# Keys and queries projected first, attention's parts laid between the gate's and u's projections of a tile

## The chip, the cores and the metric

The kernel runs on one core of one Trainium2 chip. The metric is the device time of one execution in microseconds; a time given for several runs is their median. The profiled execution is one more run, with its own time.

## The reference

Two layers (DEPTH = 2) work on 512 prompt rows and 64 sample rows of width 1024, in fp32. What matters here is the first half of a layer, the mixer:

```python
h = x @ w_in          # columns: q 512 | k 128 | v 128 | u 512 | gv 512
q, k = rope(q), rope(k)
a = sink_attention(q, k, v)      # 8 query heads, 2 key heads, head_dim 64, window of 128 + own chunk
b = gelu(u) * (tril(W_s[g]) @ LN(gelu(gv)) + bias[g])       # 4 groups of 128 channels, chunks of 128
mixed = concat(rms_norm(a), rms_norm(b)) @ w_o
x = layer_norm(ALPHA * x + mixed)
# then: router, 16 experts in 4 groups, top 2 in the best group, x = layer_norm(ALPHA * x + moe(x))
```

Besides both outputs, the rotated keys, the values and (for the samples) the normalised gate rows are returned.

## The kernel before

**Tiles.** Rows are five tiles of 128: four of the prompt, and one with the 64 sample rows and 64 rows of zeros. NT is 5. A weight matrix is streamed in units of 512 x 512 values (1 MB), four blocks of 128 rows each; for keys and values a unit is 512 x 256. A unit s goes to slot s % 4 of `raw` by a DMA of the SP queue. ScalarE rounds it to `w_hi` (`split_hi`, L376) and VectorE writes the remainder to `w_lo` (`split_lo`, L382). Every fp32 product is three matmuls in a faster format: hi*hi, hi*lo and lo*hi. So a tile's product with two units is 24 matmuls on 128x512 (`product`, L1469 to L1483). The left operand is treated in the same way: rows are transposed by TensorE (four transposes of 128x128 into one bank, `turn`, L1462 to L1467), ScalarE copies the bank to the hi part (L392), VectorE subtracts (L397).

**Units of a layer.** 0 and 1: gate (gv). 2 and 3: keys and values. 4 and 5: queries. 6 and 7: u. 8 to 11: w_o. Then six per expert.

**Order on TensorE.** `head` (L1498) turns the five tiles of x and projects the gate, tile by tile. Then, for all five tiles each, keys and values, queries, u (L1514 to L1516). Only then attention begins: the keys are turned (`kt0`, `kt1`), the gating matrices (`wst`), and a loop over t (NT + 3 rounds) staggers the tiles: `scores(t)`, `turn_queries(t + 1)`, the gating products (all in round 0), `output(t - 3)`, `weighted_values(t - 1)`, `turn_mixed(t - 2)`, `turn_x1(t - 3)`, with the router's logits two rounds behind. `output` is the product with w_o.

**Order on the others.** ScalarE and VectorE have their own lists in the same order, each strictly in sequence; an instruction that waits for a semaphore holds back all behind it. ScalarE: gelu of gate and u out of PSUM (L706), queries' hi part (`queries_out`), eight exponentials of 128x256 per tile (`exponentials`, L743), copies of the turned probabilities (`probs_out`), sums of squares, square roots. Changing between gelu, exponential and square root costs an ACT_TABLE_LOAD. VectorE: rotation of keys and queries (L978), statistics and norm of the gate (L1023 to L1062), `scores_out` (scale and mask, row maxima, L1078), `attention_out`, `gmlp_out` (one channel group of four tiles at a time), `rms_norm`, `mixed_out` (adding the w_o product to x), `layer_norm` (L1134), and the subtractions for every lo part.

**Banks and memory.** PSUM has eight banks, A to H; `fill_plan` (L64 on) counts which value fills which bank in which order, and every producer waits until the bank's last reader has freed it. Projections go round A to D. The transposed x (`xt_hi`, `xt_lo`) fills an arena that is reused, once projecting is over, for keys, split queries (`q_hi`, `q_lo`), two buffers of probabilities, the mask (a 128x3x256 tensor loaded by ScalarE's queue, L727) and others. The mixed rows' split parts (`mt_hi`, `mt_lo`) have one buffer, over the gate's rows.

**Queues of the DMAs.** SP issues the weight units in order. POOL issues the small tables at the start and per layer, stores keys and values, later gathers rows and scatters results for the experts.

The lines that hold the order of TensorE before:

```python
for g in (1, 2, 3):
    for t in range(NT):
        projection(l, g, t)
...
for t in range(NT + 3):
    if t < NT:
        scores(t)
```

Of the kernel before, what the change touches and what calls it, by code (L numbers as in the profile page):

```python
# [19 lines left out]
F32R = mybir.dt.float32r  # L20
# [42 lines left out]
def fill_plan():  # L63
# [13 lines left out]
    for g in range(4):  # L77
        for t in range(NT):
            fill(("proj", g, t), "ABCD"[(g * NT + t) % 4])
    fill("kt0", "E")  # L80
    fill(("qt", 0), "G")
    fill("kt1", "F")
    fill("wst", "H")
    for t in range(NT + 3):
        if t < NT:
            for j in range(4):
                fill(("s", t, j), "ABCD"[j])
        if t + 1 < NT:
            fill(("qt", t + 1), "H")
        if t == 0:  # L90
            for r in range(NT):
                fill(("gm", r), "GH"[r % 2])
        if 4 <= t < NT + 2:
            fill(("logit", t - 4), "H")
            fill(("turned logit", t - 4), "H")
        if t >= 3:
            for c in range(2):
                fill(("wo", c, t - 3), "AB"[c])
        if 1 <= t < NT + 1:
            for j in range(4):  # L100
                fill(("pt", t - 1, j), "EF"[j % 2])
            fill(("o", t - 1), "G")
        if 2 <= t < NT + 2:
            for h in range(2):
                fill(("mt", t - 2, h), "EF"[h])
        if 3 <= t < NT + 1:
            for h in range(2):
                fill(("rt", t - 3, h), "CD"[h])
    for t in (NT - 2, NT - 1):
        for h in range(2):  # L110
            fill(("rt", t, h), "CD"[h])
        fill(("logit", t), "H")
        fill(("turned logit", t), "H")
# [9 lines left out]
def build(nc, x_prompt, x_sample, cache_k, cache_v, w_in, sinks, gm_ln_g, gm_ln_b, gm_ws, gm_bs,  # L123
# [5 lines left out]
    with ctx:  # L129
# [10 lines left out]

        raw = sb("raw", [P, RB, 4, HALF])
        w_hi = sb("w_hi", [P, RB, 4, HALF], F32R)
        w_lo = sb("w_lo", [P, RB, 4, HALF], F32R)
        x = sb("x", [P, NT, D])
# [7 lines left out]
        small = sb("small", [P, 400])  # L152
# [6 lines left out]
        xt_hi = over(base_t, "xt_hi", [P, KT_N, ROWS], F32R)  # L159
        xt_lo = over(base_t, "xt_lo", [P, KT_N, ROWS], F32R, 4 * KT_N * ROWS)  # L160
        keys_hi = over(base_t, "keys_hi", [P, 7 * P], F32R)
        keys_lo = over(base_t, "keys_lo", [P, 7 * P], F32R, at=3584)
        q_hi = over(base_t, "q_hi", [P, 4, P], F32R, at=7168)
        q_lo = over(base_t, "q_lo", [P, 4, P], F32R, at=9216)
        probs = over(base_t, "probs", [P, 2, 4, 2, 256], at=11264)
        probs_t = over(base_t, "probs_t", [P, 2, 4, P], at=27648)
        mask = over(base_t, "mask", [P, 3, 256], at=31744)
        ws_t = over(base_t, "ws_t", [P, 4, P], at=34816)
        consts = over(base_t, "consts", [P, 3 * P + 46 + 8 * NT])
        x1_t = over(base_t, "x1_t", [P, KT_N, P], at=36864)  # L170

        logits_t = over(base_t, "logits_t", [NE, P], at=3584)
# [9 lines left out]
        mt_hi = over(base_m, "mt_hi", [P, KT_N, P], F32R, at=2 * QB)  # L182
        mt_lo = over(base_m, "mt_lo", [P, KT_N, P], F32R, at=2 * QB + 4 * D)
        squares = over(base_m, "squares", [P, HALF], at=2 * QB + 8 * D)
# [31 lines left out]
        w12, warm = sm(NT, 2), sm(3)  # L216

# [19 lines left out]
        in_slot = over(base_t, "in_slot", [P, 2, 2 * NT, P], BF16, at=11264)  # L237
# [32 lines left out]
        ws_in, mask_in, consts_in = sem("ws_in"), sem("mask_in"), sem("consts_in")  # L270
# [76 lines left out]
        def width(s):  # L347
            return 256 if s in (2, 3) else HALF
# [51 lines left out]
        def t_cols(buf, h, c):  # L400

            return buf[:, 4 * h:4 * h + 4, c * P:(c + 1) * P]
# [30 lines left out]
        def _(sp):  # L433
# [33 lines left out]
            with sp.Fori(0, DEPTH) as l:  # L467
                s = 0
                for c0, n in ((1280, HALF), (HALF, 256), (0, HALF), (768, HALF)):
# [3 lines left out]
                for c in range(2):  # L473
                    for k in range(2):
# [1366 lines left out]
```

## Time and profile before

| | us |
|---|---|
| median of 3 runs | 1302.72 |
| lowest and highest | 1291.38 and 1303.28 |
| the profiled execution, its own time | 1304.67 |
| its span, first to last instruction | 1302.7 |
| TensorE busy | 1061.4 |
| VectorE busy | 898.7 |
| ScalarE busy | 709.3 |

Times in the rows are microseconds from the start of the span. Layer 0's mixer takes from about 19 to 276 us, its experts to about 626; layer 1's mixer starts at about 645 and its experts end at 1260. In layer 1 the projections end at 757, the first w_o product starts at 803 and the last ends at 896.7. PE is TensorE, PEld its weight loads, DVE VectorE, ACT ScalarE, SP the queue of the weight units. PEclk is the granted clock of TensorE: 1.00 is 2.4 GHz, 0.50 is 1.2 GHz.

### The profile page before, as it was taken

The page shows a single profiled execution, that of the slowest core. Times are in us where ns is not written, and L with a number is a line of the kernel's source. Part 1 is how long each engine was busy: PE and PEld are TensorE (multiplying, and loading weights), DVE is VectorE, ACT ScalarE, POOL GpSimd, SP SyncE. Part 2 cuts the span into 40 slices and gives each one's busy share as a digit, 9 for nine tenths or more (in the row PEclk, how much of TensorE's full clock was granted, in tenths as well). Part 3 has the DMA queues.
Part 4 walks back from the last instruction along what each step waited for, and adds up shares of the span by engine and source line. Part 5 has one row for each costly group of instructions (what it writes and reads, how often), then busy time and mean ns, then how long its engine had stood idle before and what let it go on. Part 6 is the DMA issues. An engine that isn't in the chain of part 4 may idle for free.

```text
span 1302.7 us, 16517 instructions
## 1 busy us (share of the span) xinstructions
PE 1061.4 (81%) x5382; PEld 875.0 (67%) x5382; DVE 898.7 (69%) x1082; ACT 709.3 (54%) x857; POOL 222.5 (17%) x164
## 2 busy tenths in 40 slices
PE   4998789947699999998279987997369999999920
PEld 3887677736577777877169856875258787777810
DVE  2583764476588788786767556645667888888827
ACT  2423563254477677775432257522457787777722
POOL 3000000006121222210250000000431212111115
PEclk9999799967899999999589988998589999999975
DMA  9313100026799999998713202011297999999851
GB/s 294 131 71 98 66 33 24 33 81 222 248 373 360 359 358 367 363 359 306 281 49 137 85 13 81 17 41 69 80 327 269 367 376 372 369 382 372 312 189 56
DMA packets 115618, 273.22 MB, mean 210 GB/s; under 512 B 10016, under 2 KB 13056, under 8 KB 114400
## 3 DMA queue, kind: packets, MB, share of 16 engines
q1 hardware_dynamic: 98608, 227.36, 48.8%
q0 software_dynamic: 14336, 33.00, 7.2%
q10 hardware_dynamic: 2608, 12.06, 2.6%
q8 instruction: 33, 0.54, 0.2%
q14 instruction: 33, 0.27, 0.1%
HBM read 262.00 MB, written 25.22 MB: 220 GB/s over the span
## 4 chain that ended last, share of the span: by engine, by line
PE 36%; DMA 20%; DVE 16%; issue 13%; ACT 8%; POOL 3%; DVEq 2%; POOLq 1%; ACTq 0%; SPq 0%
DMA raw<-in_w_gate 15%; PE bankA L1477 8%; PE bankB L1477 8%; DVE w_lo L382 5%; ACT w_hi L376 4%; PE bankC L1477 4%; PE bankD L1477 3%; DVE xt_lo L397 3%; POOL slot_rows L605 2%; PE bankA L1686 2%; PE bankB L1686 2%; PE bankC L1709 2%; PE bankD L1709 1%; DVE x L1405 1%; DMA rows<-x_rows,idx 1%
## 5 line engine op out<-in xcount | busy, mean ns | idle before, releaser
L382 DVE TENSOR_TENSOR w_lo<-raw,w_hi 128x2048 fp32r<-128x2048 f32 x216 | 487.7, 2269 | 111.8 <-ACT w_hi L376 110.2
L376 ACT ACTIVATE w_hi<-raw 128x2048 fp32r<-128x2048 f32 x216 | 409.7, 1901 | 214.1 <-DMA raw<-in_w_gate 54.6
L1686 PE MATMUL bankA<-w_hi,xt_hi 128*128 128x512 f32 x256 | 103.0, 402 | 18.8 <-DVE xt_lo L397 18.8
L1686 PE MATMUL bankB<-w_hi,xt_hi 128*128 128x512 f32 x256 | 102.6, 401 | 0.0
L1686 PE MATMUL bankB<-w_hi,xt_lo 128*128 128x512 f32 x256 | 100.1, 391 | 0.0
L1686 PE MATMUL bankA<-w_hi,xt_lo 128*128 128x512 f32 x256 | 100.1, 391 | 0.0
L1686 PE MATMUL bankB<-w_lo,xt_hi 128*128 128x512 f32 x256 | 99.8, 390 | 0.0
L1686 PE MATMUL bankA<-w_lo,xt_hi 128*128 128x512 f32 x256 | 99.7, 390 | 0.0
L585 POOL DMA_INDIRECT rows<-x_rows,idx x28 | 51.3, 1832 | 263.2 <-PE bankF L1466 225.4
L591 POOL DMA_INDIRECT y_rows<-expert_out,idx x32 | 54.1, 1691 | 221.0 <-ACT expert_out L853 221.0
L1686 PEld LDWEIGHTS bankA<-w_hi,xt_hi 128*128 128x128 f32 x256 | 48.3, 189 | 38.4 <-issue 29.2
L397 DVE TENSOR_TENSOR xt_lo<-bankE,xt_hi 128x512 fp32r<-128x512 f32 x42 | 28.8, 686 | 61.5 <-ACT xt_hi L392 61.5
L392 ACT ACTIVATE xt_hi<-bankE 128x512 fp32r<-128x512 f32 x42 | 24.5, 584 | 85.5 <-PE bankE L1466 55.3
L1709 PE MATMUL bankC<-w_hi,xt_hi 128*128 128x512 f32 x128 | 53.5, 418 | 3.3 <-DVE xt_lo L397 3.3
L1466 PE MATMUL bankE<-ident,rows 128*128 128x128 f32 x128 | 22.2, 302 | 40.7 <-DMA rows<-x_rows,idx 20.6
L1686 PEld LDWEIGHTS bankB<-w_hi,xt_lo 128*128 128x128 f32 x256 | 48.0, 188 | 10.5
L1686 PEld LDWEIGHTS bankA<-w_hi,xt_lo 128*128 128x128 f32 x256 | 48.0, 188 | 10.4
L1686 PEld LDWEIGHTS bankA<-w_lo,xt_hi 128*128 128x128 f32 x256 | 48.4, 189 | 9.2
L1686 PEld LDWEIGHTS bankB<-w_lo,xt_hi 128*128 128x128 f32 x256 | 48.2, 188 | 9.2
L1686 PEld LDWEIGHTS bankB<-w_hi,xt_hi 128*128 128x128 f32 x256 | 48.1, 188 | 9.1
L1709 PE MATMUL bankC<-w_hi,xt_lo 128*128 128x512 f32 x128 | 51.0, 398 | 0.0
L1709 PE MATMUL bankC<-w_lo,xt_hi 128*128 128x512 f32 x128 | 50.8, 397 | 0.0
(321 smaller groups left out, 2486.0 us busy)
## 6 DMA issues: line engine op xcount, KB each, us to landing
raw<-in_w_gate SPq DMA_DIRECT2D x64, 1024.0 KB, 8.2
raw<-in_w_up SPq DMA_DIRECT2D x64, 1024.0 KB, 7.8
raw<-in_w_down SPq DMA_DIRECT2D x64, 1024.0 KB, 7.1
raw<-in_w_in SPq DMA_DIRECT2D x12, 1024.0 KB, 8.9
raw<-in_w_o SPq DMA_DIRECT2D x8, 1024.0 KB, 5.8
y_rows<-y_rows ACTq DMA_DIRECT2D x8, 1024.0 KB, 8.5
x_rows<-x POOLq DMA_DIRECT2D x10, 512.0 KB, 3.0
raw<-in_w_in SPq DMA_DIRECT2D x4, 512.0 KB
```

The lines of the kernel that those rows point to most:

```text
L376: act.activation(w_hi[:, s % RB, :, 0:n], raw[:, s % RB, :, 0:n], ACT.Copy).then_inc(hi_done, 1)
L382: dve.tensor_tensor(w_lo[:, s % RB, :, 0:n], raw[:, s % RB, :, 0:n], w_hi[:, s % RB, :, 0:n].bitcast(F32), ALU.subtract).then_inc(lo_done, 1)
L392: act.activation(dst, bank_of(name)[:, :].rearrange("p (k n) -> p k n", k=4), ACT.Copy).then_inc(s, 1)
L397: read(dve.tensor_tensor(lo, bank_of(name)[:, :].rearrange("p (k n) -> p k n", k=4), hi.bitcast(F32), ALU.subtract), name)
L585: pool.indirect_dma_start(out=rows[:, e % 2, :], out_offset=None, in_=x1_dram, in_offset=bass.IndirectOffsetOnAxis(ap=src.bitcast(U32), ax ...
L591: pool.indirect_dma_start(out=y2_dram, out_offset=bass.IndirectOffsetOnAxis(ap=idx[:, e, 0:1].bitcast(U32), axis=0), in_=expert_out[:, e % ...
L605: pool.indirect_dma_start(out=slot_dram, out_offset=bass.IndirectOffsetOnAxis(ap=slots[:, c:c + 1].bitcast(U32), axis=0), in_=ints[:, c, : ...
L1405: dve.scalar_tensor_tensor(out=x[0:n, t, :], in0=y_rows[0:n, t % YB, 1, :], scalar=w12[0:n, t, 1:2], in1=x[0:n, t, :], op0=ALU.mult, op1=A ...
L1466: ins = pe.transpose(bank_of(name)[:, k * P:(k + 1) * P], src, ident)
L1477: ins = pe.matmul(out, a[:, k, col:col + P], w[:, slot, j, 0:n], start=(m == 0 and a is a_hi and w is w_hi), stop=(m == len(steps) - 1 and ...
L1686: ins = pe.matmul(out, a[:, 4 * k + t, (c % 2) * P:(c % 2 + 1) * P], w[:, (s + k) % RB, t, :], start=(k == t == 0 and a is xt_hi and w is ...
L1709: ins = pe.matmul(bank_of(f"down{h}")[:, :], a[:, 2 * j + r, cols], w[:, (s + j) % RB, 2 * r + h, :], start=(j == r == 0 and a is xt_hi an ...
```

## The change

1. **Units.** The order of the units is now keys and values (0, 1: 512 x 256), queries (2, 3), gate (4, 5), u (6, 7), then w_o.
2. **Head.** For each tile of x: the key/value product, then the query product, with the next tile's transposes between. Their banks go round A, B, C, D, G, H. In VectorE's list rotating keys and queries comes after all five row subtractions.
3. **Halved products.** `product` becomes `half_product`: one unit, 12 matmuls; each unit is waited for by itself.
4. **Merged loop.** For each tile t the gate's product (bank A) and u's product (bank B) are issued in halves, and between the halves stand scores of tile t-1 (banks C, D), and transposed probabilities and values of tile t-2. Gating is now per tile: four matmuls of 128x128 for each tile, and the first stands in the loop.
5. **End.** After the loop: gating 1 to 3 and scores 4, attention of tiles 3 and 4, then w_o products in two halves of columns, between them the mixed rows' transposes, logits and x's transposes.
6. **Memory.** x^T is laid out by tile (`xt[P, NT, 2, KT, P]`), so that a projected tile's room can be reused; probabilities have five buffers, two over `raw` slots 0 and 1, three over x^T of tiles 2 to 4; `q_hi` and `q_lo` lie over `raw` slot 2. So w_o's units are loaded as 8, 9, 11, 10, with 8 waiting for the last probability transpose of tile 0, 9 for that of tile 1 and 10 for the last scores of tile 4. `mt` has two buffers.
7. **Mask.** It is 128x3x8 values, broadcast over 64 columns, loaded once by POOL with six small DMAs at the start; the 384 KB load is gone.

```diff
-                for c0, n in ((1280, HALF), (HALF, 256), (0, HALF), (768, HALF)):
+                for c0, n in ((HALF, 256), (0, HALF), (1280, HALF), (768, HALF)):
...
+                for s, free in ((8, ("pt", 0, 3)), (9, ("pt", 1, 3)), (11, None), (10, ("s", NT - 1, 3))):
+                    if free is not None:
+                        wait_filled(sp, free, l)
+                        sp.sem_inc(held_sp, 1)
+                    c, k = (s - UNITS_PROJ) // 2, s % 2
+                    load(l, s, w_o[l, k * HALF:(k + 1) * HALF, c * HALF:(c + 1) * HALF])
...
+            for m in range(3):
+                for a in range(2):
+                    pool.dma_start(mask[:, m, 4 * a:4 * a + 4], c_mask[m, :, 0::64], allow_slow_non_contiguous=True).then_inc(boot, 16)
```

ScalarE's list, from the merged loop on:

```diff
+                for t in range(1, NT):
+                    gelu(2, gv, t)
+                    if t >= 2:
+                        probs_out(t - 2, range(2))
+                        if t == NT - 1:
+                            split_hi(act, l, 8)
+                        probs_out(t - 2, range(2, 4))
+                    gelu(3, u, t)
...
+                    queries_out(t)
+                    exponentials(t - 1)
+                    if t == 2:
+                        gate_spread(0, 2)
+                    if t == 3:
+                        gate_spread(2, 4)
+                split_hi(act, l, 9)
+                gate_spread(4, NT)
+                sums_of_squares(0)
+                sums_of_squares(1)
+                split_hi(act, l, 10)
+                probs_out(3, range(4))
+                mixed_hi(0)
                 split_hi(act, l, 11)
...
+                exponentials(4)
+                probs_out(4, range(4))
+                sums_of_squares(2)
+                mixed_hi(1)
```

VectorE's:

```diff
+                for t in range(NT):
+                    keys_out(t)
+                    if t == NT - 1:
+                        split_lo(dve, l, 4)
+                        split_lo(dve, l, 5)
+                    rotated_queries(t)
+                split_lo(dve, l, 6)
+                split_lo(dve, l, 7)
...
+                for t in range(1, NT):
                     if t >= 3:
...
+                        attention_out(t - 3)
+                    scores_out(t - 1)
+                    gate_stats(t)
+                    if t == 3:
+                        gate_scale(0, 2, 1)
+                        gate_norm(0)
+                        gate_norm(1)
+                    if t == 4:
+                        split_lo(dve, l, 8)
+                        gate_scale(2, 4, 2)
+                        gmlp_out(0)
+                        gate_norm(2)
+                        gate_norm(3)
+                        split_lo(dve, l, 9)
+                    queries_lo_out(t)
+                gmlp_out(1)
+                attention_out(2)
+                scores_out(4)
...
+                mixed_out(0)
+                layer_norm(0)
+                attention_out(4)
+                rms_norm(2)
```

TensorE's:

```diff
+                for t in range(NT):
+
+                    projection(l, 2, t, 0)
+                    if t:
+                        scores(t - 1, (0, 1))
+                    projection(l, 2, t, 1)
+                    if t:
+                        scores(t - 1, (2, 3))
+                    if t >= 2:
+                        turn_probs(t - 2, (0, 1))
...
+                    projection(l, 3, t, 0)
+                    if t >= 2:
+                        values(t - 2, 0)
+                        values(t - 2, 1)
+                        turn_probs(t - 2, (2, 3))
+                    projection(l, 3, t, 1)
+                    if t >= 2:
+                        values(t - 2, 2)
+                        values(t - 2, 3)
...
+                    turn_queries(t)
+                gmlp(1)
+                scores(NT - 1, (0, 1))
+                gmlp(2)
+                scores(NT - 1, (2, 3))
+                gmlp(3)
...
+                attention_end(NT - 2)
+                turn_mixed(0)
+                output(0, 0)
+                attention_end(NT - 1)
+                gmlp(4)
+                turn_mixed(1)
+                output(0, 1)
+                for t in range(1, NT):
+                    output(t, 0)
+                    if t + 1 < NT:
+                        turn_mixed(t + 1)
...
+                    output(t, 1)
+                    turn_x1(t - 1)
```

## Rows read from the trace of the kernel before

**Rows 1.** The page: TensorE's busy time; the two splits by line.

```profile
PE 1061.4 (81%) x5382; PEld 875.0 (67%) x5382; DVE 898.7 (69%) x1082; ACT 709.3 (54%) x857; POOL 222.5 (17%) x164
...
L382 DVE TENSOR_TENSOR w_lo<-raw,w_hi 128x2048 fp32r<-128x2048 f32 x216 | 487.7, 2269 | 111.8 <-ACT w_hi L376 110.2
L376 ACT ACTIVATE w_hi<-raw 128x2048 fp32r<-128x2048 f32 x216 | 409.7, 1901 | 214.1 <-DMA raw<-in_w_gate 54.6
```

**Rows 2.** Stretches of layer 1: start:end, length, engines' busy time (count), PEclk, DMA.

```profile
645.00:688.00 43.00, 35.99 (x153) 29.27 (x154) 28.62 (x50) 16.62 (x22) 21.25 (x17) 0.85 0.26 82
...
757.00:803.00 46.00, 32.19 (x231) 26.02 (x229) 32.64 (x53) 31.04 (x86) 0.74 (x1) 0.85 0.19 67
803.00:897.00 94.00, 89.31 (x520) 74.90 (x521) 50.92 (x89) 35.57 (x86) 2.73 (x5) 0.98 0.07 26
```

**Rows 3.** Waits of TensorE, 757 to 897: total us, times, longest.

```profile
PE bankG L1542 <- ACT probs_t L740: 5.3, 6, 4.0
PE bankH L1570 <- DVE q_lo L397: 3.6, 1, 3.6
PE bankA L1477 <- DVE probs L1087: 3.3, 1, 3.3
```

**Rows 4.** Chain that ended last: start us, us, what. Products, transposes, values.

```profile
192.69 5.68 PE bankA L1477 x24
198.37 5.44 PE bankB L1477 x24
...
228.94 0.84 PE bankG L1542 x8
...
669.07 0.44 PE bankE L1466 x4
...
688.15 2.87 PE bankB L1477 x24
```

**Rows 5.** Busy time by stretch, line L1560 alone: scores of one tile.

```profile
760.60:762.70 2.10, 2.03 (x24) 1.83 (x24) 1.00 0.02 4
```

**Rows 6.** Instructions at the kernel's start: start us, us, engine, line, what.

```profile
10.37 1.91 ACT L376 ACTIVATE w_hi<-raw 128x2048 fp32r<-128x2048 f32 x1 [2.40 <-DMA raw<-in_w_in]
...
17.91 1.07 POOL L533 DMA_DIRECT2D rope<-in_c_rope  x1 [15.66 <-DMA x<-in_x_prompt]
...
18.99 0.77 PE L1477 MATMUL bankA<-w_hi,xt_hi 128*128 128x512 f32 x1 [11.65 <-issue]
```

**Rows 7.** The same for VectorE at the head of layer 1.

```profile
658.25 0.69 DVE L397 TENSOR_TENSOR xt_lo<-bankE,xt_hi 128x512 fp32r<-128x512 f32 x1
```

**Rows 8.** The same: key work of one tile.

```profile
696.82 0.29 DVE L1039 COPY kv<-bankD 128x128 f32<-128x128 f32 x1
...
697.36 0.21 DVE L987 TENSOR_TENSOR rope_b<-bankD,rope 128x64 f32<-128x64 f32 x1
```

**Rows 9.** The same for ScalarE: exponentials of one tile, first and last.

```profile
795.06 1.28 ACT L747 ACT_TABLE_LOAD   x1
796.35 0.51 ACT L747 ACTIVATE probs<-probs,small 128x256 f32<-128x256 f32 x1
...
800.31 0.20 ACT L749 ACTIVATE small<-small 128x8 f32<-128x8 f32 x1
```

**Rows 10.** The same for TensorE: gating products around a wait.

```profile
763.10 1.02 PE L1570 MATMUL bankG<-gv,ws_t 128*128 128x512 f32 x2
767.74 2.07 PE L1570 MATMUL bankH<-gv,ws_t 128*128 128x512 f32 x2 [3.62 <-DVE q_lo L397]
```

**Rows 11.** Busy time by stretch: clock behind that wait.

```profile
770.00:773.00 3.00, 3.00 (x4) 0.91 (x3) 1.36 (x2) 1.26 (x7) 0.00 (x0) 0.50 0.00 0
```

**Rows 12.** DMA issues, 40 to 90 us: KB each, median us to landing.

```profile
raw<-in_w_o SPq DMA_DIRECT2D x4, 1024.0 KB, 5.8
```

**Rows 13.** Chain that ended last: the last w_o eviction, then x's transpose.

```profile
896.68 0.69 DVE x L1130
...
903.10 0.82 PE bankC L1466 x4
```

More of the change, by code:

```diff
@@ L109, in fill_plan @@
-    for t in (NT - 2, NT - 1):
+    for t in range(NT):
+        for g in range(2):
+            fill(("proj", g, t), "ABCDGH"[(2 * t + g) % 6])
+    for t in range(NT):
+        fill(("proj", 2, t), "A")
+        if t:
+            for j in range(4):
+                fill(("s", t - 1, j), "CD"[j % 2])
+        fill(("proj", 3, t), "B")
+        if t >= 2:
+            for j in range(4):
+                fill(("pt", t - 2, j), "EF"[j % 2])
+            fill(("o", t - 2), "G")
+        if t == 0:
+            fill("kt0", "E")
+            fill("kt1", "F")
+        if t == 1:
+            fill("wst", "G")
+        if t == NT - 1:
+            fill(("gm", 0), "H")
+        fill(("qt", t), "H")
@@ new lines, in fill_plan @@
+    fill(("gm", 1), "D")
+    fill(("gm", 2), "H")
+    fill(("gm", 3), "B")
+    for j in range(4):
+        fill(("s", NT - 1, j), "CD"[j % 2])
+    for t in (NT - 2, NT - 1):
+        for j in range(4):
+            fill(("pt", t, j), "EF"[j % 2])
+        fill(("o", t), "G")
+        if t == NT - 2:
+            for h in range(2):
+                fill(("mt", 0, h), "EF"[h])
+    fill(("gm", 4), "H")
+    for t in range(1, NT):
+        for h in range(2):
+            fill(("mt", t, h), "EF"[h])
@@ L110, in fill_plan @@
+    for t in range(NT):
+        for c in range(2):
+            fill(("wo", c, t), "AB"[c])
         for h in range(2):
@@ L151, in build @@
         ident = sb("ident", [P, P])[:, :]
-        small = sb("small", [P, 400])
+        small = sb("small", [P, 420])
         ints = sb("ints", [P, 2 * NT, 2], I32)
@@ L216, in build @@
         w12, warm = sm(NT, 2), sm(3)
+        mask = sm(3, 8)
         shared = sm(4 * NT * 6)
@@ L347, in width @@
         def width(s):
-            return 256 if s in (2, 3) else HALF
+            return 256 if s in (0, 1) else HALF
         def wait_half(act, l, s, i=0):
@@ L472, in _ @@
                         s += 1
-                for c in range(2):
-                    for k in range(2):
-                        load(l, s, w_o[l, k * HALF:(k + 1) * HALF, c * HALF:(c + 1) * HALF])
-                        s += 1
+                for s, free in ((8, ("pt", 0, 3)), (9, ("pt", 1, 3)), (11, None), (10, ("s", NT - 1, 3))):
[4 more added lines that the diff above has]
+                    load(l, s, w_o[l, k * HALF:(k + 1) * HALF, c * HALF:(c + 1) * HALF])
                 gate_up(l, SO_MOE, 0)
@@ L1549, in turn_queries, with scores @@
                     turn(("qt", t), l, [q[:, t, j * P:(j + 1) * P] for j in range(4)])
-                def scores(t):
-                    wait_read(pe, ("qt", t), l)
+                def scores(t, js):
+                    if js[0] == 0:
+                        wait_read(pe, ("qt", t), l)
                     k0 = t * P if t < NT - 1 else 5 * P
-                    for j in range(4):
+                    for j in js:
                         name = ("s", t, j)
@@ new lines, in _, with attention_end @@
+                    if t == 1:
+                        pe.wait_ge(tril_done, l + 1)
+                        turn("wst", l, [ws[:, g, :] for g in range(4)])
+                        wait_read(pe, "kt1", l)
+                        pe.sem_inc(held_pe, 1)
+                    turn_queries(t)
[4 more added lines that the diff above has]
+                gmlp(3)
+                def attention_end(t):
+                    turn_probs(t, (0, 1))
+                    values(t, 0)
+                    values(t, 1)
+                    turn_probs(t, (2, 3))
+                    values(t, 2)
+                    values(t, 3)
@@ L1744, in turned, with three_pass @@
                         ins.then_inc(ov_pe, 1)
-                    def three_pass(out, col, units, after):
+                    def three_pass(out, n, units, after):
                         pe.wait_ge(ov_dve, ran * DVE_STEPS + after)
```

484 lines of the change are left out of this document (203 added, 281 removed).

## The prediction

> **What bounds the kernel now.** I read the page first, then stages, then waits. Over the span TensorE is busy 81% [rows 1]; nothing is bound by one engine throughout, so the stages decide. The change touches two stretches, one per layer, from the first product to the last w_o product: 19.0 to 261.8 us, and 645.4 to 896.7 us. The stage table [rows 2] shows where TensorE is unfilled: 43 us at the head of layer 1 (36.0 busy, clock 0.85), 46 us of attention (32.2 busy, clock 0.85), and 94 us of w_o, almost full. In attention it waits for softmax's copies and subtractions: 5.3 us in six waits (one of 4.0), and single ones of 3.6 and 3.3 [rows 3].
>
> Pure work of a stretch at full clock, as the new order needs it, from the chain's pieces [rows 4]: 25 wide products of 24 matmuls at 5.44 and 5 narrow at 2.87 (150.4 us); 55 groups of four transposes at 0.44 (24.2); scores 2.1 per tile (10.5) [rows 5]; values 0.84 per pair of heads with two key blocks (15.1); gating about 0.95 per tile (8 instructions at the transposes' 0.11 each: 4.8, an estimate); three logits groups (5.5). Together about 211, against 242.8 and 251.3 now. So 32 and 40 us per layer are waits and half clock, and the question is how much the new order keeps.
>
> **The change, step by step.** Let T be the moment when the head's last row transpose ends. At T, three tiles of keys and queries are done.
>
> *T in layer 0.* Now unit 0 (1 MB) is split at 10.37 and the first product starts at 18.99, when both units are split [rows 6]. After, the first two units hold half as much, units 2 and 3 are needed before the first query product, and x's later rows are requested earlier, behind unit 1. I place keys of tile 0 at 11.2 to 17.1 (half clock), the query halves at 18.7 and 22.2 as their units are split, tile 0's end at 25.2; then 0.9 of transposes, 1.3 for copy and subtraction, two tiles of 2.87 + 5.44 and the other transposes: T = 46.7, give or take 2. POOL issues six small mask loads before it releases x's tiles 2 to 4; at up to the 1.07 of its first issue [rows 6] that is 6.4 us, and those tiles are wanted only at 30: nothing.
>
> *T in layer 1.* x comes tile by tile out of the previous tail, which is unchanged. Start 645.4; keys at half clock 5.8, queries 5.4, transposes 0.9; tile 1's subtraction stands in VectorE's queue behind the tail's work, which puts it at 658.25 now [rows 7]; some 0.4 later then, ready at 659.9. Keys, transposes, queries, keys, transposes, queries, transposes: T = 679.2. TensorE does 8.3 us per tile instead of 5.4, so it absorbs x's lateness.
>
> *T to Q, the last query transpose.* VectorE may evict tile 0's keys only after the last row subtraction: hi and lo 1.35, then key work read out after 1.1 [rows 8]; the fourth key product needs that bank: 2.4 us of wait. All other work: two tiles of keys and queries 16.6, ten products 54.4, scores of four tiles 8.4, transposed probabilities and values of three 13.8, other transposes 3.3, one gating 1.0. Q = T + 100. Hidden here: per tile ScalarE's gelus, copies, eight exponentials (with a table load 5.35, from 795.06 to the end of 800.31) [rows 9] and reloads take some 14 us beside 18; its tightest copy is 1.3 us early. VectorE's query subtraction is 1.5 early after two gate norms. Splits of units 4 to 7 finish just ahead of their product. If that cover goes, see the slow rivals.
>
> *Q to S, the last scores.* Here the order on the queues bites. The last query subtraction stands on VectorE behind unit 9's subtraction; that waits for ScalarE's split of unit 9, behind the exponentials of tile 3, behind Q. So 0.55 + 5.35 + 1.9 + 2.3 + 0.65 [rows 1, 9] = 10.8, of which TensorE fills 1.0: **a wait of about 9.9 us**. A wait of 3.6 was enough for a half-speed stretch: one gating product took 2.07 instead of 1.02 [rows 10], at a granted clock of 0.50, the 1.2 GHz level [rows 11]. At that rate the two score pairs and gating 2 take 6.1 (full clock: 4.6, by VectorE's copies). S = Q + 17.
>
> *S to the first w_o product.* q's split halves lie over raw unit 2's slot, so w_o's unit 10 is requested only at S. It lands in 5.8 [rows 12], is split in 1.9, and only behind it does ScalarE copy the probabilities that the values of tile 3 need: 0.3 + 5.8 + 1.9 + 0.5 = 8.5, of which 2.5 is filled: **a second wait, 6 us**. Values at half clock, the mixed transposes, their copy and subtraction: first output product at S + 18.3.
>
> *The rest.* Ten products 54.4, tile 4's attention 5.3 with 1.5 of waits (exponentials behind unit 11's split), gating 1.0, transposes 6.3, logits and their turns 6.1. One more wait: tile 2's norm stands on VectorE behind tile 0's layer norm, which ends 6.4 after its product (896.68 to 903.10) [rows 13]: 3.4, and 1.5 for the clock. Last product at S + 97.7.
>
> *Handoffs.* A product behind another kind of work takes 5.68 instead of 5.44, behind transposes about nothing [rows 4]. Halved products give some 18 extra returns: between 0.5 and 4.3 per layer. I take 1.8, most returns being from transposes.
>
> At nothing: the mask load leaves ScalarE's queue (its issue there hid behind the last projection; uncovered some 0.4 us, as the issues on that queue in general); table loads are about as many; the rows' transposed copies are laid out by tile, but every instruction keeps its shape; w_o's units 8, 9 and 11 are requested behind transposes that are done by T + 80, and are wanted at S + 18. Behind the last product both kernels do the same: the last layer norm ends 6.4 after it, then router and experts. The experts' first loads move later, from ahead of attention to S, still 90 us ahead of use.
>
> **Sum.** T + 100 + 17 + 97.7 + 1.8 = T + 216.5, taken as 217. Layer 0: 263.7 against 261.8, +1.9. Layer 1: 896.2 against 896.7, -0.5. Together +1.4 on the profiled run's own 1304.67 us (span 1302.7): 1306. That run is 1.95 above the median of 1302.72; I forecast **1304**. The new order fills the old gaps and makes two larger ones.
>
> The Trainium skill (ScalarE: Activation LUTs, "What ACT_TABLE_LOAD costs") gives about 2.66 us for each switch, a 1283 ns load and a 1380 ns drain. The trace has the load, but an exponential starts 1.3 us after the load did, so no drain shows behind it here; by the page the sum would be near 1318 (third rival).
>
> **The rivals.**
> *Faster, 1280.* The stretch behind S runs full: VectorE and ScalarE have caught up in the long waits, and the clock stays up. Then 6 us of lesser waits (1.3 + 1.5 + 3.4) and 6 us of half clock per layer vanish: -24. For it: the w_o stage is nearly full now [rows 2]. Against: clock fell after every wait of 3.3 us or more that I followed, and the norm's place in the queue is fixed. 0.25.
> *Slower, 1319.* The handoffs cost 0.24 each, and unit 10 lands late, because the experts' loads are issued right behind it: 2.5 + 5 us more per layer, 15 in all. It decides from a landing near 10 us, against the 5.8 seen on an idle queue. 0.14.
> *Slower, 1318: table switches.* If a switch costs twice the load that the row shows, ScalarE is late in the merged loop: three switches per tile, 3.9 more, against 1.3 us of slack in tile 3 and 2.3 in tile 4; plus one switch on each later chain (Q to S, tile 4's exponentials): 2.6 + 1.6 + 2.8 = 7 per layer. It decides from 0.45 us extra a switch. Against: [rows 9]. 0.10.
> *The change does not do what it says:* nothing speaks for it; the two waits are in the order itself. 0.01.
>
> **How the numbers follow.** Forecast 0.50, faster 0.25, the slow ones 0.24 together. Within 1% (13 us, about what a measurement of this kernel can tell from no change) are all of the forecast's case but 0.06 at its ends, and 0.03 of the faster one: 0.47; faster 0.25, slower 0.28. The bounds add up to: low, 1304 - 24, with 2 taken back because both losses must vanish whole; high, 1304 + 15 + 5 for T and the waits' lengths. The range is 1282 to 1324; it leaves out about 0.12 below (the far side of the faster rival) and 0.06 above. The likeliest case's own: 1294 to 1314.
>
> **What would show it.** Right: in each layer one TensorE wait near 10 us before the last tile's scores, released by VectorE's q_lo; one near 6 before tile 3's values, released by probs_t; the attention mixed in the projections without waits over 1 us; half clock after both. Wrong: those waits under 5 us, or waits on probs_t, q_lo or gelu in each tile of the merged loop; T later than 49 or 681; the last w_o product more than 5 us from T + 217.

## The result, and the profile after

The changed kernel takes **1329.7 us** (median of 4 runs, 1322.9 to 1333.4) against 1302.1 for the kernel before in the same comparison: a ratio of 1.0226, interval [1.0176, 1.0276]. The forecast was 1304, its range 1282 to 1324. The profiled execution has a span of 1330.4 us, 27.7 more than before.

The page after: engines, the two splits [rows 1], and TensorE and its clock in 40 slices of 33.3 us.

```profile
PE 1083.9 (81%) x5430; PEld 897.7 (67%) x5430; DVE 905.7 (68%) x1110; ACT 718.9 (54%) x865; POOL 224.0 (17%) x170
...
PE   6999688956699999997379995998269999999920
...
PEclk9999869977899999999689996889599999999975
...
L394 DVE TENSOR_TENSOR w_lo<-raw,w_hi 128x2048 fp32r<-128x2048 f32 (+1 forms) x216 | 488.2, 2268 | 119.8 <-ACT w_hi L388 118.3
L388 ACT ACTIVATE w_hi<-raw 128x2048 fp32r<-128x2048 f32 (+1 forms) x216 | 409.9, 1901 | 192.1 <-DMA raw<-in_w_gate 54.1
```

The splits cost what they did. TensorE was given the same products and is busy 22.5 us longer: its instructions became slower, by the clock and, as will be seen, by handoffs. Slices 5 and 6 (133 to 200 us) are where layer 0's attention ends.

The five stretches of layer 1 after: head to T, T to Q, Q to S, S to the first w_o product (O1 below), O1 to the last (E). Columns as in [rows 2].

```profile
653.90:689.30 35.40, 32.39 (x176) 28.96 (x176) 23.11 (x29) 10.29 (x15) 20.31 (x16) 0.89 0.31 101
689.30:798.80 109.50, 103.56 (x601) 87.81 (x601) 70.01 (x164) 52.09 (x101) 2.84 (x5) 0.97 0.10 33
798.80:816.50 17.70, 7.66 (x42) 6.80 (x40) 8.25 (x15) 12.77 (x32) 0.00 (x0) 0.67 0.01 1
816.50:836.50 20.00, 13.62 (x66) 12.75 (x65) 10.85 (x22) 6.23 (x8) 0.00 (x0) 0.59 0.58 210
836.50:920.70 84.20, 80.49 (x404) 66.24 (x405) 45.27 (x79) 25.02 (x58) 4.59 (x8) 0.92 0.15 55
```

Between Q and O1 TensorE is busy for 21 of 38 us, at a clock of 0.67 and 0.59. TensorE's waits in the same 267 us (compare [rows 3]):

```profile
PE bankC L1591 <- DVE q_lo L409: 10.0, 1, 10.0
PE bankA L1514 <- DVE rope_b L1002: 5.7, 1, 5.7
PE bankG L1572 <- ACT probs_t L736: 5.3, 3, 4.8
PE bankA L1514 <- DVE xt L409: 5.3, 1, 5.3
PE bankE L1501 <- DVE q L1120: 3.2, 1, 3.2
```

All three waits that the forecast named are there: 9.9 was forecast, 10.0 came; 6 and 4.8; 3.4 and 3.2. `rope_b` was forecast at 2.4 (2.3 in layer 0).

The stages, from the first starts and last ends of TensorE's instructions:

| stage | forecast | layer 0 | layer 1 |
|---|---|---|---|
| layer's first product to T | T at 46.7; 33.8 in layer 1 | T at 45.7 | 35.4 |
| T to Q | 100 | 106.0 | 109.5 |
| Q to S | 17 | 17.7 | 17.7 |
| S to O1 | 18.3 | 20.6 | 20.0 |
| O1 to E | 79.4 | 82.2 | 84.2 |
| handoffs, beside the above | 1.8 | in the rows above | in the rows above |

Layer 0's last product ends at 272.3 (forecast 263.7, before 261.8), 8.6 over the forecast. Layer 1's stretch is 266.8 (forecast 250.8, before 251.3), 16.0 over. Outside the two stretches the profiled run is 2.0 shorter between the layers and 3.7 longer behind E. 8.6 + 16.0 - 2.0 + 3.7 = 26.3, and the 1.4 forecast: 27.7.

### The profile page after: what moved, and what is told of

Same layout as the page of the kernel before. It is cut to its first block, busy times and chain, and to the rows that moved or that the text cites. A ratio compares the mean times of both kernels' runs of the same rounds, so it can differ in the third digit from the quotient of the medians.

```text
span 1330.4 us, 16998 instructions
## 1 busy us (share of the span) xinstructions
PE 1083.9 (81%) x5430; PEld 897.7 (67%) x5430; DVE 905.7 (68%) x1110; ACT 718.9 (54%) x865; POOL 224.0 (17%) x170
## 4 chain that ended last, share of the span: by engine, by line
PE 37%; DMA 22%; DVE 17%; issue 11%; ACT 6%; DVEq 3%; POOL 3%; POOLq 1%; SPq 0%; ACTq 0%
DMA raw<-in_w_gate 13%; PE bankB L1514 9%; PE bankA L1514 7%; DVE w_lo L394 6%; ACT w_hi L388 5%; PE bankG L1572 3%; DVE xt L409 2%; POOL slot_rows L623 2%; PE bankA L1742 2%; PE bankE L1501 2%; PE bankC L1765 2%; PE bankD L1765 1%; PE bankB L1742 1%; DMA raw<-in_w_down 1%; PE bankF L1501 1%
## 5 line engine op out<-in xcount | busy, mean ns | idle before, releaser
L394 DVE TENSOR_TENSOR w_lo<-raw,w_hi 128x2048 fp32r<-128x2048 f32 (+1 forms) x216 | 488.2, 2268 | 119.8 <-ACT w_hi L388 118.3
L388 ACT ACTIVATE w_hi<-raw 128x2048 fp32r<-128x2048 f32 (+1 forms) x216 | 409.9, 1901 | 192.1 <-DMA raw<-in_w_gate 54.1
L1742 PE MATMUL bankA<-w_hi,xt 128*128 128x512 f32 x512 | 166.4, 396 | 17.5 <-DVE xt L409 17.1
L1742 PE MATMUL bankB<-w_hi,xt 128*128 128x512 f32 x512 | 166.3, 396 | 0.0
L1742 PEld LDWEIGHTS bankA<-w_hi,xt 128*128 128x128 f32 x512 | 96.3, 188 | 47.5 <-issue 28.1
L1742 PEld LDWEIGHTS bankB<-w_hi,xt 128*128 128x128 f32 x512 | 96.2, 188 | 19.5
L1742 PE MATMUL bankA<-w_lo,xt 128*128 128x512 f32 x256 | 99.8, 390 | 0.0
L1742 PE MATMUL bankB<-w_lo,xt 128*128 128x512 f32 x256 | 99.8, 390 | 0.0
L1765 PE MATMUL bankC<-w_hi,xt 128*128 128x512 f32 x256 | 93.9, 408 | 4.4 <-DVE xt L409 4.3
L1765 PE MATMUL bankD<-w_hi,xt 128*128 128x512 f32 x256 | 89.6, 391 | 0.0
L1514 PE MATMUL bankB<-w_hi,xt 128*128 128x512 f32 x224 | 74.5, 398 | 4.0 <-DVE w_lo L394 4.0
L1514 PEld LDWEIGHTS bankA<-w_hi,xt 128*128 128x128 f32 x224 | 44.2, 209 | 26.4 <-issue 10.4
L1765 PEld LDWEIGHTS bankD<-w_hi,xt 128*128 128x128 f32 x256 | 48.2, 188 | 10.3
```

Source lines behind the costliest of these rows:

```text
L388: act.activation(w_hi[:, s % RB, :, 0:n], raw[:, s % RB, :, 0:n], ACT.Copy).then_inc(hi_done, 1)
L394: dve.tensor_tensor(w_lo[:, s % RB, :, 0:n], raw[:, s % RB, :, 0:n], w_hi[:, s % RB, :, 0:n].bitcast(F32), ALU.subtract).then_inc(lo_done, 1)
L1514: ins = pe.matmul(bank_of(name)[:, 0:n], part[:, 4 * k0 + j, :], w[:, s % RB, j, 0:n], start=(k0 == j == 0 and part is hi and w is w_hi), ...
L1742: ins = pe.matmul(out, a[:, c % 2, 4 * k + t, :], w[:, (s + k) % RB, t, :], start=(k == t == 0 and a is xt_hi and w is w_hi), stop=(k == 1 ...
L1765: ins = pe.matmul(bank_of(f"down{h}")[:, :], a[:, n, 2 * j + r, :], w[:, (s + j) % RB, 2 * r + h, :], start=(j == r == 0 and a is xt_hi an ...
```

## The experiments

Three theories, of causes that can all be there at once. **Queue**: each excess is a place in VectorE's or ScalarE's list, and moving one entry takes one wait away. **Clock**: TensorE's idle time brings a half-clock stretch that costs as much again. **Handoffs**: the halved products and the alternation cost it, whatever the queues do; no run takes this one alone, and it is read from the trace. e1 to e3 move one entry each, e4 all three; e5 another; e6 and e8 keep the waits and fill them; e7 puts together what helped; e9 repeats the changed kernel.

### e1: queries first

```diff
                         gate_norm(3)
-                        split_lo(dve, l, 9)
                     queries_lo_out(t)
 ...
                 scores_out(4)
+                split_lo(dve, l, 9)
```

> Unit 9's subtraction moves on VectorE's queue from before the last query subtraction (q_lo of tile 4) to behind the last scores' copies; nothing else changes. My theory: the 10.0 us wait of TensorE before tile 4's scores, in each layer, is that place in the queue and nothing else. It should vanish from the waits (under 1 us left), the time from the last query transpose to the last scores should fall from 17.7 to 7 to 8 us, and the kernel should be 20 to 22 us faster than the changed kernel, about 1309. Rival A: what the wait hid comes out behind it. ScalarE still has tile 3's exponentials and unit 9's split to do, so the probabilities of tile 3 come no sooner and the second wait (4.8 us, released by probs_t) grows by what the first one loses: then a gain of 0 to 8 us. Rival B: the excess over the forecast (26 us) is handoffs between kinds of products, and the wait was covering for catching up; then the gain is half or less.

Measured: 1310.0 us, ratio to the kernel before 1.0075 [1.0036, 1.0114], 1.5% (20 us) below the changed kernel's 1.0226. Q to S is 6.8 us in both layers; the wait on `q_lo` is down from 10.0 to 1.6 (under 1 was expected). But part of rival A came too. TensorE's first wait in layer 1:

```profile
PE bankG L1572 <- ACT probs_t L736: 7.5, 3, 7.0
```

S to O1 became 21.1 in both layers (from 20.6 and 20.0): ScalarE's work had not moved, and its copy is waited for 7.0 us instead of 4.8.

### e2: probabilities first

```diff
-                split_hi(act, l, 10)
                 probs_out(3, range(4))
                 mixed_hi(0)
+                split_hi(act, l, 10)
 ...
-                split_lo(dve, l, 10)
                 mixed_lo(0)
+                split_lo(dve, l, 10)
```

> ScalarE copies the transposed probabilities of tile 3 and the mixed values of tile 0 before it splits unit 10, and VectorE subtracts the mixed values of tile 0 before unit 10's subtraction; the rest is as in the changed kernel. My theory: the 4.8 us wait before tile 3's values is the landing of unit 10 (5.6 and 4.9 us) and its split (1.9), with the copy queued behind both. Without it the values start at once and at full clock: S to the first w_o product falls from 20.6 and 19.9 to about 13 us, 14 to 18 us for the kernel, if unit 10 is split by the time its product comes; unit 10's split then ends about 8 to 9 us behind S, which leaves room. Rival A: the first w_o product then waits for units 8 to 10 or for the mixed values' subtraction instead: a gain under 6 us. Rival B: the half clock behind the first, 10.0 us wait stays, and values still run at 1.2 GHz: a gain of 8 to 10.

Measured: 1316.4 us, 1.0113 [1.0070, 1.0155], 15 us less than the changed kernel. S to O1 fell to 10.3 and 10.1 us, further than I had said, and with 2.00 us per pair of values, at full clock, right behind the 10.0 us wait. Rival B is wrong. But in layer 0 O1 to E grew from 82.2 to 89.0. The first instruction of tile 4's values there, and the ten microseconds around it:

```profile
190.33 0.55 PE L1572 MATMUL bankG<-cache,probs_t 128*128 128x64 f32 x2 [2.76 <-DVE q L1081]
```

```profile
190.00:200.00 10.00, 9.67 (x45) 9.44 (x46) 1.69 (x4) 4.10 (x8) 0.00 (x0) 0.53 0.59 203
```

A wait of 2.8 us on VectorE (tile 3's attention stood behind two splits) and a clock of 0.53: rival A in a place where I had not looked. VectorE's list is the same in layer 1, but there the first w_o product ran partly at half clock (7.35 us instead of 5.77), so TensorE came to the wait later and stood 1.3 us.

### e3: keys early

```diff
             for t in range(NT):
+                if t == NT - 1:        # layer 0; in the tail likewise, ahead of tile 4's rows
 ...
+                    keys_out(0, 0)
+                    rotated_queries(0, 0)
                 rows_lo_x(0, t)
 ...
-                for t in range(NT):
-                    keys_out(t)
+                for t in range(1, NT):
+                    keys_out(l, t)
```

> VectorE takes tile 0's keys and rotated queries out of their banks before the last row subtraction of the head instead of behind it, in both layers; the rest is as in the changed kernel. My theory: behind the head's last row transpose (T) VectorE is the pacer: keys and rotation cost 3.6 us per tile, and four unit splits stand between, so that the first u product starts 26.8 us behind T. Starting one tile (3.6 us) earlier should take away the waits of 2.3 and 5.7 us on the first bank and bring T to Q down from 106.0 and 109.4 us to 101 to 104: 8 to 12 us for the kernel. Rival A: the last row subtraction is now late by the same 3.6 us, T moves out by it and the sum stays: a change under 3 us. Rival B: the excess of T to Q over the forecast 100 us is in the products (handoffs) and not in VectorE: under 3 us also, but with T where it was.

Measured: 1313.4 us, 1.0144 [1.0061, 1.0226], 11 us less, with an interval too wide to lean on; the stages carry it. T stayed (35.8 and 35.2 us behind the layer's first product), T to Q fell from 106.0 and 109.5 to 102.5 and 105.3. Layer 1 stays 1.3 us above the 101 to 104 that were expected. So VectorE, not the handoffs, held 3.6 and 4.2 us.

What layer 1 still has over layer 0 is in VectorE's list: last row subtraction and next instruction, in the changed kernel and then in e3.

```profile
690.18 0.68 DVE L409 TENSOR_TENSOR xt<-bankF,xt 128x512 fp32r<-128x512 f32 x1
694.25 0.29 DVE L1039 COPY kv<-bankA 128x128 f32<-128x128 f32 x1 [3.40 <-issue]
```

```profile
683.11 0.68 DVE L409 TENSOR_TENSOR xt<-bankF,xt 128x512 fp32r<-128x512 f32 x1
686.26 0.29 DVE L1029 COPY kv<-bankC 128x128 f32<-128x128 f32 x1 [2.48 <-issue]
```

VectorE waits for nothing that the profile shows. In e3 tile 0's keys already lie ahead, another instruction follows, and the gap is still there: it belongs to the place, the edge of the loop over layers. Where the loop is entered for layer 0 the copy of tile 0's keys starts at 47.13 us, right behind the subtraction. In the gap of the changed kernel (690.5 to 694.3 us) the core's DMA queue of the kind "instruction" moved packets:

```profile
q14 instruction: 4, 0.03, 3.2%
```

This queue moved four in e3's gap too (683.0 to 686.3), and none from 46.5 to 50.5 us in layer 0. That the gap is VectorE waiting for its instructions is a likely reading, but no run changed it, and it is not shown.

### e4: all three

> All three edits together. My theory: they take away different idle stretches of TensorE, and the half clock behind the first two goes as well, so that the gains add up: 40 to 48 us less than the changed kernel, 1282 to 1290 us, below the kernel before (1302). If the waits only pass on to one another (rivals A of the three), the sum is well below the three single gains, and the time stays above 1300.

Measured: 1298.8 us, 1.0009 [0.9977, 1.0040]. The forecast was missed. The single gains add up to 3.5% (1.51 + 1.13 + 0.82), the three together bring 2.2%. T to Q and Q to S keep their gains (102.5 and 104.9; 6.8 and 8.0), but S to O1 is 17.0 in both layers, not e2's 10. TensorE's waits in layer 0 behind 60 us, and ScalarE ahead of the copy:

```profile
PE bankG L1578 <- ACT probs_t L736: 5.2, 1, 5.2
PE bankE L1507 <- DVE q L1123: 3.2, 1, 3.2
PE bankG L1578 <- DVE q L1084: 2.8, 1, 2.8
```

```profile
154.87 1.90 ACT L388 ACTIVATE w_hi<-raw 128x2048 fp32r<-128x2048 f32 x1
156.78 1.28 ACT L769 ACT_TABLE_LOAD   x1
...
161.17 0.63 ACT L755 ACTIVATE ws<-u 128x512 f32<-128x512 f32 x1
...
162.17 0.58 ACT L736 ACTIVATE probs_t<-bankE 128x512 f32<-128x512 f32 x1
```

The copy now stands behind unit 9's split, a table load and two tiles' sums of squares, 7.3 us from 154.87. In e2 TensorE's 10 us wait had hidden these. In layer 1 the wait is only 2.2 us, and the clock from S to O1 is 0.60 (0.80 in layer 0). So the waits do pass on to one another, by about a third. The whole times alone would hardly tell 3.5% from 2.2%, with intervals this wide; the stage does: 7 us per layer are 1.0% in all.

### e5: norm first

```diff
+                attention_out(4)
+                rms_norm(2)
                 mixed_out(0)
                 layer_norm(0)
-                attention_out(4)
-                rms_norm(2)
```

> On VectorE's queue tile 4's attention_out and tile 2's rms_norm stand ahead of tile 0's mixed_out and layer_norm instead of behind them; the rest is as in the changed kernel. My theory: the 3.2 us wait of TensorE before the transposes of tile 2's mixed values, in each layer, is VectorE working on tile 0's layer norm; with the norm ahead of it the wait goes, and with it part of the half clock behind it: first w_o product to last falls from 82.2 and 84.2 us to 77 to 80, 6 to 11 us for the kernel. Rival A: the layer norm that now comes later delays x of tile 0, its transposes and router rows, or the release of the bank of the first output product, and the wait moves there: a change under 3 us. Rival B: only the 3.2 us go and the clock in the stretch does not change: 6 us.

Measured: 1309.5 us, 1.0123 [1.0057, 1.0189], 13 us less than the changed kernel. The norm's wait is gone from both layers; O1 to E is 76.9 and 75.2 us. That is 5.3 and 9.0 us less, 14 together, more than the expected 6 to 11. Two waits of 3.2 are 6.4, about half of it; no other wait of that size went. The other half I take for clock: from O1 to E it is 0.98 and 1.00, against 0.96 and 0.92. Rival A is wrong, and rival B by the stages: the interval of the whole time would not tell 6 us from 13.

### e6 and e8: the waits filled

```diff
                 gmlp(1)
+                wait_free(pe, ("s", NT - 1, 0), l)
+                for n in range(84):          # e8: 88
+                    pe.transpose(bank_of(("s", NT - 1, 0))[:, 0:P], ident, ident)
                 scores(NT - 1, (0, 1))
 ...
                     turn_probs(t, (0, 1))
+                    if t == NT - 2:
+                        wait_free(pe, ("o", t), l)
+                        for n in range(40):      # e8: 58
+                            pe.transpose(bank_of(("o", t))[:, 0:P], ident, ident)
```

> The changed kernel with TensorE kept busy in its two long waits: 84 transposes of the identity into the bank that the next scores use (10.0 us wait), and 40 into the bank of the next values (4.8 us wait); at 0.11 us each they take some 9.3 and 4.4 us. They compute nothing that is read. No wait is shortened. My theory: half clock behind the waits is a price of its own, beside the waits: values of tile 3 took 3.67 and 3.51 us a pair instead of 2.0, the first w_o product 7.56 and 8.56 instead of 5.44. Filled, the granted clock stays at 1.0 up to the first w_o product, S to the last w_o product falls by 5 to 7 us per layer, and the kernel is 10 to 14 us faster though it does more work. Rival A: the clock falls anyway (it follows something else than TensorE's idle time): no gain, under 3 us. Rival B: the dummies overrun the waits (a transpose at half clock takes 0.22 us): slower by 5 to 15 us.

> As e6, with 88 and 58 transposes in place of 84 and 40, to close what was left of the waits (0.8 and 2.0 to 2.2 us, the latter with TensorE idle from 173.5 to 175.7). In e6 the clock stayed at 1.00 through the first fill and up to 175, S came 2.3 and 1.0 us sooner, and the clock fell to 0.50 behind the 2.2 us that was still idle. My theory: idle time before the fall, not the kind of work, brings the half clock. With both waits closed the values take 2.0 us instead of 3.67 and S to the first w_o product falls from 20.2 and 17.3 us to 14 to 16; the kernel is 8 to 14 us faster than the changed kernel of the same call. Rival A: the clock falls at 176 again although TensorE was busy: then S to the first w_o product stays at 20 and the kernel within 4 us of the changed one. Rival B: the clock stays up there but falls later in the w_o stage, at the norm's wait (3.2 us): S to the first w_o product shorter, the last w_o product less so, a gain of 3 to 8 us.

> The changed kernel as it is, once more, so that the filled one is compared on the same chip and the spread of its stages from execution to execution is seen. My theory: 1.018 to 1.028 of the kernel before, with the waits of 10.0 and 4.8 to 5.9 us in the same places in both layers, and T to Q at 106 and 109.5 us within 0.5. Rival: the stretches of the first record were an unlucky execution; then T to Q, which has no half clock in it, comes nearer the forecast 100.

e6 measured 1322.3 us, 1.0204 [1.0137, 1.0272]: no gain that can be told from none, and the forecast was missed. The second fill ended 2.2 us too soon, and the clock fell there (stretches of e6: 170 to 175 and 175 to 180):

```profile
170.00:175.00 5.00, 3.52 (x33) 3.28 (x31) 4.42 (x15) 1.72 (x1) 0.00 (x0) 1.00 1.03 393
175.00:180.00 5.00, 4.28 (x23) 4.28 (x24) 2.45 (x2) 1.40 (x4) 0.00 (x0) 0.63 0.69 245
```

e8 closes it. Layer 0 from 150 to 200 us, the changed kernel once more (e9) and then e8:

```profile
150.00:200.00 50.00, 33.09 (x159) 29.31 (x157) 28.75 (x55) 26.48 (x61) 1.85 (x3) 0.66 0.30 112
```

```profile
150.00:200.00 50.00, 46.83 (x370) 43.37 (x369) 31.46 (x62) 32.87 (x74) 1.84 (x3) 1.00 0.40 130
```

A clock of 1.00 (2.4 GHz) instead of 0.66. The same values, in the changed kernel's first record and in e8:

```profile
177.91 3.67 PE L1572 MATMUL bankG<-kv,probs_t 128*128 128x64 f32 x16 [4.76 <-ACT probs_t L736]
```

```profile
176.61 2.00 PE L1572 MATMUL bankG<-kv,probs_t 128*128 128x64 f32 x16 [0.24 <-ACT probs_t L736]
```

e8 has 292 matmuls more than e9 and takes 1315.4 us, 1.0132 [1.0087, 1.0177], against e9's 1331.6, 1.0251 [1.0209, 1.0293], on the same chip: 16 us less, somewhat above my 8 to 14. S to O1 is 16.3 and 16.0 us. Rival A is wrong. Part of rival B came: from O1 to E, where the norm's wait is left, the clock is 0.98 and 0.96. By stages, Q to O1 is 31.6 and 31.2 us instead of 37.8 and 37.7, O1 to E 80.4 and 82.0 instead of 84.0 and 84.0. So in this stretch the half clock followed TensorE's idle time, and cost 6.3 and 6.5 us per layer ahead of O1, 3.6 and 1.9 behind it.

e9 did as expected: 10.0 us waits, `probs_t` 5.1 and 5.0, T to Q 106.0 and 109.5. The excess is no accident of one record.

### e7: the ends reordered

```diff
                 split_hi(act, l, 9)
+                probs_out(3, range(2))
                 gate_spread(4, NT)
                 sums_of_squares(0)
+                probs_out(3, range(2, 4))
                 sums_of_squares(1)
-                split_hi(act, l, 10)
-                probs_out(3, range(4))
                 mixed_hi(0)
-                split_hi(act, l, 11)
                 exponentials(4)
-                probs_out(4, range(4))
+                probs_out(4, range(2))
+                split_hi(act, l, 10)
+                probs_out(4, range(2, 4))
+                split_hi(act, l, 11)
```

> The edits of e1 (queries first), e3 (keys early) and e5 (norm first) together, and a new order behind the last scores: ScalarE copies the first half of tile 3's probabilities right behind unit 9's split, the second half behind tile 0's sums of squares, then the mixed values of tile 0, tile 4's exponentials ahead of the splits of units 10 and 11; VectorE norms tile 0 ahead of the gates of tiles 2 and 3, and takes tile 3's attention out before both subtractions. My theory: in the kernel with all three edits (e4) the rest of the loss is a 5.2 us wait on probs_t before tile 3's values (two sums of squares stand ahead of the copy), 2.8 us before tile 4's values and 3.2 us for the norm, with half clock behind them. Without them S to the first w_o product falls from 17.0 to 11 to 13 us, and the kernel is 15 to 24 us below e4's 1299 (against the kernel before about 0.984), 1275 to 1284. Rival A: tile 4's exponentials ahead of the splits make output product 1 of tile 0 wait for unit 10 or 11: a gain under 6 us. Rival B: the clock, not the waits, sets the stretch, and falls elsewhere: a gain of 8 us or less.

VectorE's list follows suit: tile 0's norm ahead of the gates of tiles 2 and 3, tile 3's attention out, gate 4 and norm 1 ahead of both subtractions.

Measured: **1279.9 us** (10 runs), ratio to the kernel before 0.9887 [0.9856, 0.9919]: below both kernels, as expected. TensorE's waits in layer 1 (622 to 865 us) after those of the head:

```profile
PE bankG L1580 <- ACT probs_t L736: 2.5, 4, 1.8
PE bankA L1522 <- DVE w_lo L394: 2.4, 1, 2.4
PE bankA L1522 <- DVE mt L409: 1.6, 1, 1.6
PE bankC L1599 <- DVE q_lo L409: 1.6, 1, 1.6
```

None is over 2.4 us. S to O1 is 11.9 and 13.9 (11 to 13 was expected), O1 to E 78.3 and 78.8; layer 0's last product ends at 246.1 (before 261.8) and layer 1's stretch is 242.6 (before 251.3). Rival A is wrong; of rival B only this much came, that half clock is not gone. From Q to S, in layer 0 and in layer 1:

```profile
149.20:155.90 6.70, 5.14 (x41) 4.37 (x39) 5.67 (x14) 6.67 (x20) 0.00 (x0) 1.00 0.01 2
762.50:771.50 9.00, 7.43 (x42) 6.38 (x40) 5.93 (x14) 7.82 (x20) 0.00 (x0) 0.71 0.01 2
```

The clock is 1.00 and 0.71, and from S to O1 it is 1.00 and 0.74. TensorE is idle for about as long in both layers (5.7 and 5.2 us from Q to O1, no wait over 2.1), yet only layer 1 ran partly at half clock there, and it took 4 us more. So long waits are not the only thing that half clock follows, and these runs do not show what else does.

## Why the prediction was wrong

**What held.** The structure did: the places, releasers and lengths of the three waits, T within 1.6 us, the copy of the probabilities behind unit 10's split, and half clock behind both long waits. The new order brought waits of 10.0, 4.8 and 3.2 us per layer, where the old one's longest was 4.0 [rows 3], and e1, e2 and e5 show that each was an entry in a list.

**What failed: the clock's price (the largest part), VectorE's list behind T, and the size of the handoffs.** The chain that ended last in layer 1 after, in order (start, length, what; compare [rows 4]):

```profile
690.75 3.39 issue
...
712.62 2.29 DVE w_lo L394
717.12 2.30 DVE w_lo L394
719.54 5.74 PE bankB L1514 x24
726.38 2.77 PE bankA L1514 x12
730.40 2.95 PE bankA L1514 x12
...
768.10 2.75 PE bankB L1514 x12
...
816.85 4.91 DMA raw<-in_w_o
...
824.31 3.68 PE bankG L1572 x16
829.69 3.51 PE bankG L1572 x16
836.49 8.56 PE bankA L1514 x24
...
869.21 7.40 PE bankB L1514 x24
```

- *"Splits of units 4 to 7 finish just ahead of their product"*, the cover for VectorE behind T: wrong. VectorE sets the start of the first u product. I had it at T + 24.4 (two tiles of keys and queries 16.6, the gate product 5.44, the wait 2.4); it is at T + 26.8 and T + 30.2: 2.4 and 5.8 us over. Before unit 6 is ready stand five tiles' key work and rotation at 3.6 us each and the subtractions of units 4, 5 and 6 at 2.3. With the steps between them VectorE takes 25.2 us in both layers (47.13 to 72.31, 694.25 to 719.41), without waiting for anyone. I had priced the first bank's wait and not added up the list behind it. The 3.3 us by which layer 1 is worse is the gap at the loop's edge (3.40), which no row of mine covered: before, VectorE sat waiting for a gelu there, so a gap would have cost nothing. e3 took 3.6 and 4.2 us back by starting the list earlier. Behind the 5.7 us wait layer 1 has half clock too (0.92 from 695.1 to 719.5 us, against 1.00 in layer 0; the expectation of e9 is wrong there), but VectorE's list hid it.
- *Handoffs, 1.8*: from the first u product to Q it took 79.3 us in both layers, where the working leaves 75.6. TensorE is busy all through it at a clock of 1.00. That is 3.7 in this stretch alone, 1.9 more than taken and inside the bounds of 0.5 to 4.3. The halves beside scores take 2.77 and 2.95 us (2.72 would be half of 5.44), and a pair of scores occupies 1.25 us, from the first row here to the second, so 2.5 per tile where [rows 5] gave 2.1. No experiment undoes the halves, so this term is measured but its cause is argued:

```profile
761.56 0.38 PE L1591 MATMUL bankC<-keys_hi,q_hi 64*128 64x256 f32 x1
...
762.81 0.50 PE L1514 MATMUL bankA<-w_hi,xt 128*128 128x512 f32 x1
```

- *"Values at half clock"*: I had the state, at too small a price, and let it end there. The first w_o product still took 7.56 and 8.56 us instead of 5.44, and after the norm's wait one took 7.1 and 7.4. Q to S was 0.7 over, S to O1 2.3 and 1.6, O1 to E 2.8 and 4.8: 5.8 and 7.1 per layer. The waits themselves were not longer than forecast, so this excess is nearly all clock; w_o products between transposes took 5.67 us where the working has 5.44, which adds some tenths. By filling two of the three waits e8 took back 9.9 and 8.4 us of it, and not all. I had taken about 5.4 for the whole: 3.9 up to O1 (35.3 against e8's 31.4 at full clock) and 1.5 behind the norm.
- Together for layer 0: 2.4 + 1.9 + 5.8 - 1.0 (T) = 9.1; 8.6 seen. Layer 1: 5.8 + 1.9 + 7.1 + 1.6 = 16.4; 16.0 seen. (The forecast had rounded up by 0.5.)

**The rivals.** *Faster, 1280*: the stretch behind S did not run full by itself. e7 comes to that rival's number, 1280, but by reordered lists, and with half clock left in layer 1. *Slower, 1319*: one of its two parts came. The handoffs cost 1.9 more per layer, of its 2.5, but unit 10 did not land late: 5.6 and 4.9 us. *Slower, table switches*: wrong, and in the merged loop TensorE never waits for ScalarE. ScalarE at tile 3's exponentials after:

```profile
152.38 1.28 ACT L743 ACT_TABLE_LOAD   x1
153.67 0.51 ACT L743 ACTIVATE probs<-probs,small 128x256 f32<-128x256 f32 x1
```

The first exponential starts 1.29 us behind the load's start. The Trainium skill (ScalarE: Activation LUTs, "What ACT_TABLE_LOAD costs") adds a drain to the load; this trace shows none, and the measurement decides.

**The chances.** Forecast and faster rival had 0.75 together. The working had two longer waits in it, and at each step took the price at which the next engine had just kept up. Where a new order lengthens a wait, the bound upwards is the wait with its half clock, and the list behind it added up entry by entry; with 8 us for these per layer, 16 in all, the upper end of 1324 would have been 1340, above the 1329.7 measured. That number is known only now; the step that was left out, adding up the list, was open to me then.

**Left open.** Whether VectorE's 2.5 to 3.4 us at the loop's edge are the fetching of its instructions. What brings half clock without a long wait, as in e7's layer 1 but not in its layer 0. And what the halved products cost by themselves.

## What to carry to other kernels

When attention is laid into projections, the engine that fills the gaps is not the one to check first: add up each helper's list between two points where TensorE must have its result, with every weight split in it. An entry that can wait (a weight's split, a layer norm) must stand behind the ones for which TensorE is idle; reordered lists turned a kernel 2.3% slower than its predecessor into one 1.1% faster. Remove the waits together, and look at the list again after each: taken one by one their gains were 3.5%, together 2.2%, until the next entries were moved as well.

## What the runs showed of the hardware

- Useless matmuls in a long wait can pay. 292 transposes in e8 made the kernel 1.2% faster, because the granted clock from 150 to 200 us stayed at 1.00 where it was 0.66 on average. Filling all but 2.2 us of the second wait (e6) did not. But half clock also came in e7's layer 1 (0.71 and 0.74 from Q to O1), where no wait was over 1.8 us.
- VectorE stood idle for 3.40 us at the edge of the loop over layers (2.48 in e3), with no wait shown and four packets of an instruction queue in the gap; it did not when the loop was entered.
- A 12-matmul half next to scores took 2.77 to 2.95 us, next to transposes or values 2.75, against half of 5.44.
